# The second token tile's MoBA attention moved between the expert picks of the first tile

## The reference

```
x = x + rwkv7_time_mix(rms_norm(x))                       # block 1, layer A
k, v = shared keys and values of rms_norm(x) @ w_kv        # 16 heads of 64, block 1, layer B
q, gate = split(rms_norm(x) @ w_in)
o = softmax(mask(q k^T / 8)) v                             # causal: one MoBA block holds all 256 tokens
x = x + (o * silu(gate)) @ w_out
h = concat(16 meta tokens, x)                              # block 2
h = h + (sigmoid(g) * rg_lru(...) @ w_rnn + sigmoid(g') * mla_attention(...) @ w_att) @ w_out
h = h + peer(rms_norm(h))                                  # 8 heads x top 16 of 16384 experts, u and v rows gathered
out = rms_norm(h)[16:]
```

## Time and profile before

| | |
|---|---|
| median of 3 runs | 1422.13 us (1419.67 to 1423.77) |
| profiled execution, time | 1427.83 us |
| profiled execution, span | 1426.0 us |
| mean granted TensorE clock | 0.907 |
| busy in the span: TensorE, VectorE, ScalarE, GpSimd | 83%, 62%, 36%, 20% |
| bytes moved | 414.93 MB, of them 269.5 MB on the gathers' queue |

### The profile page before, as it was taken

One profiled execution on the slowest core, in us unless ns is written; L12 is line 12 of the kernel. 1 busy time (PEld: TensorE's weight loads), 2 busy tenths in 40 slices (PEclk: granted clock), 3 DMA queues, 4 the chain that ended last, 5 costly groups with the idle time before them and its releaser, 6 DMA issues.

```text
span 1426.0 us, 23109 instructions
## 1 busy us (share of the span) xinstructions
PE 1188.5 (83%) x8702; PEld 795.0 (56%) x8702; DVE 886.7 (62%) x2284; ACT 508.4 (36%) x1526; POOL 287.5 (20%) x269
## 2 busy tenths in 40 slices
PE   7999998999999999999897878986666665656564
PEld 4445798987479988998675544754122222222111
DVE  7526766556563563147585487566777787777654
ACT  1214222211262143122442476324344444344334
POOL 0000000000000000001231334322354344443440
PEclk9899999999999999999998989998678778787867
DMA  8344100243324586779999999999999999999995
GB/s 314 129 150 148 47 3 3 76 158 122 119 89 131 196 301 214 238 266 399 365 421 413 394 393 379 421 420 423 413 425 425 423 426 424 424 425 426 425 425 245
DMA packets 82960, 414.93 MB, mean 291 GB/s; under 512 B 10847, under 2 KB 15327, under 8 KB 49761
## 3 DMA queue, kind: packets, MB, share of 16 engines
q0 software_dynamic: 37152, 269.50, 45.6%
q1 hardware_dynamic: 45554, 143.69, 28.4%
q10 hardware_dynamic: 144, 0.26, 0.0%
HBM read 412.36 MB, written 1.06 MB: 290 GB/s over the span
## 4 chain that ended last, share of the span: by engine, by line
PE 46%; DMA 30%; DVE 6%; issue 3%; ACT 3%; POOL 2%; POOLq 0%; DVEq 0%; ACTq 0%
DMA row<-peer_in,arena 14%; PE bank L1893 12%; DMA arena<-peer_in,arena 12%; PE bank L2915 7%; DMA ring<-stream_in 4%; PE bank L1425 3%; PE bank L1505 2%; PE bank L2803 2%; PE bank L1482 2%; PE bank L846 2%; PE bank L2081 2%; PE bank L655 1%; PE bank L645 1%; POOL arena L3235 1%; DVE arena L3193 1%
## 5 line engine op out<-in xcount | busy, mean ns | idle before, releaser
L2915 PE MATMUL bank<-arena 128*64 128x512 f32 x808 | 321.6, 765 | 153.1 <-ACT arena L3050 153.1
L3193 DVE CUSTOM_DVE_ANT_0 arena<-arena 128x1024 f32<-128x1024 f32 x202 | 246.6, 1224 | 153.7 <-DMA arena<-peer_in,arena 150.8
L3235 POOL DMA_INDIRECT arena<-peer_in,arena x202 | 219.7, 1088 | 561.3 <-PE bank L2915 371.2
L2915 PEld LDWEIGHTS bank<-arena 128*64 128x64 f32 x808 | 76.5, 160 | 323.1 <-issue 319.7
L1893 PE MATMUL bank<-arena,ring 128*128 128x128 f32 (+1 forms) x1984 | 239.8, 281 | 13.3 <-DMA ring<-stream_in 11.7
L1893 PEld LDWEIGHTS bank<-arena,ring 128*128 128x128 f32 x1984 | 232.2, 194 | 27.6 <-issue 14.5
L3034 ACT ACTIVATE arena<-arena 128x2 f32<-128x2 f32 (+1 forms) x130 | 26.4, 203 | 393.6 <-DVE arena L3193 393.5
L3038 ACT ACTIVATE arena<-arena 128x1 f32<-128x1 f32 x256 | 85.4, 380 | 4.3
L3043 ACT ACTIVATE arena<-arena 128x1 f32<-128x1 f32 x256 | 84.1, 375 | 6.8 <-DVE arena L3199 6.4
L2803 PEld LDWEIGHTS bank<-arena,ring 128*128 128x128 f32 x512 | 65.8, 209 | 34.6 <-issue 29.3
L2915 PE MATMUL bank<-row,arena 128*64 128x512 f32 x112 | 71.5, 774 | 7.1 <-ACT arena L3050 7.1
(11 more groups left out here) (395 smaller groups left out, 1856.6 us busy)
## 6 DMA issues: line engine op xcount, KB each, us to landing
ring<-stream_in SPq DMA_DIRECT2D x243, 512.0 KB, 4.7
ring<-stream_in SPq DMA_DIRECT2D x16, 384.0 KB, 5.6
arena<-peer_in,arena POOLq DMA_INDIRECT x202, 19.9
row<-rows_in SPq DMA_DIRECT2D x4, 512.0 KB, 18.2
ring<-stream_in SPq DMA_DIRECT2D x16, 128.0 KB, 7.4
cst<-cst_in SPq DMA_DIRECT2D x1, 1900.0 KB, 17.0
row<-rows_in POOLq DMA_DIRECT2D x2, 512.0 KB, 6.0
cst<-rg_w_in SPq DMA_DIRECT2D x1, 1024.0 KB, 6.7
```

Source lines behind the costliest of these rows:

```text
L2915: return nc.tensor.matmul(core.banks[2 * t + b][rows_of(j), :], diag[i % ND], places[seat[i]][:, D + b * 512:D + (b + 1) * 512], start=Fal ...
L3193: ins = nc.vector.tensor_tensor_reduce(out=row, in0=row, in1=X2[t][i % 2], scale=STEEP, scalar=0.0, op0=ALU.mult, op1=ALU.add, accum_out=d ...
L3235: pool.indirect_dma_start(out=places[seat[i]], out_offset=None, in_=g.names["peer"], in_offset=bass.IndirectOffsetOnAxis(ap=index[:, i:i + ...
```

## The change

- The attention loop of `moba` does scores, transposes and weighted sums for the first tile only; one transpose bank now holds a pair of heads. The gate and the values are still projected there for both tiles. The output projection for the second tile goes, and with it the work that ran beside it.
- Keys, queries, values and gate that the second tile still needs are written to a DRAM tensor `spill` (four tiles of 512 KB, issued by GpSimd) and read back later (`bring`) into places that the first pass of `second_mix` has freed. ScalarE, VectorE and GpSimd wait for the four writes at the start of that pass.
- The second tile's attention becomes a generator `late_pass` for TensorE, ScalarE and VectorE, in `g.late`. `experts` draws on it ahead of `g.later`, from `START` on: 25 steps, then the output projection with `out_b` loaded a second time, then the norm for `second_mix`.
- `RATE` goes from 1.2 to 2.0. In unit 6 (picks 96 to 111) VectorE takes no step of choosing unit 8 in the first five pairs of picks and eight steps a pair after them (`LATE_ROUTE`).
- The place of the gates' weights is a seat from pick 0 up to pick 39 (`DROPPED`), so there are 7 seats then; from 40 to 63 there are 6, and the 1 MB of gates' weights is loaded again; 7 from 64 (`GATED`), 12 from 116.

The diff, cut to its core:

```diff
@@ moba, TensorE
         def scores(j):
-            banks = [claim(pe, ("s_b", 2 * j + p), p) for p in range(2)]
...
-                nc.tensor.matmul(banks[p][:, P:W3], qT[p][:, P:T], kT[p], start=True, stop=True).then_inc(*full(("s_b", 2 * j + p)))
+                nc.tensor.matmul(bank[:, 0:P], rotated["qb"][rows, 0, j, :], rotated["kb"][rows, 0, j, :], start=True, stop=True).then_inc(*full(key))
...
-        for m in range(KT):
-            key = ("out_b", 1, m)
-            bank = claim(pe, key)
-            project_out(bank[:, 0:P], m, 1).then_inc(*full(key))
...
+        def late_pass():
+            pe.wait_ge(brought.handle, 64)
+            copied(pe, ("vb", 1, 1))
+            for i in range(H + 9):
+                if i < H:
+                    late_scores(i)
+                if 5 <= i < H + 5:
+                    late_turn(i - 5)
+                if i >= 9 and i % 2:
+                    late_weigh((i - 9) // 2)
+                g.at["late", i] = g.now
+                yield ("late", i), 1
+            for n in range(2):
+                copied(pe, ("o_b1", n))
+            for m in range(KT):
+                late_out(m)
+                yield 1.0
+            yield ("out_b", 1, 1), 4
+            pe.wait_ge(squared_late.handle, 2)
...
+            g.at[key] = g.now
+            yield key, 4
+        g.late["pe"] = late_pass()
@@ moba, ScalarE
+        def late_pass():
+            for i in range(H + 9):
+                yield ("late", i), 1
+                if 6 <= i < H + 6:
+                    late_keep(i - 6)
+                if 2 <= i < H + 2:
+                    late_exps(i - 2)
...
@@ moba, VectorE
-            if m >= 6:
-                for j in range(4 * m - 24, 4 * m - 20 - (m == 7)):
-                    norm_first(j)
+        copied(dve, ("ss_c", 0))
+        lk(nc.vector.reciprocal(g.rstd_c[:, 0:first], g.rstd_c[:, 0:first]))
+        for j in range(KT):
+            nc.vector.scalar_tensor_tensor(out=g.second_in[0][:, j, :], in0=tiles(g.res, S)[:, j, 0:first], scalar=vec("norm1", j),
+                                           in1=g.rstd_c[:, 0:first], op0=ALU.mult, op1=ALU.mult).then_inc(*g.normed_c.up())
+        def late_pass():
+            dve.wait_ge(brought.handle, 64)
+            for i in range(H + 9):
+                yield ("late", i), 1
+                if 1 <= i < H + 1:
+                    mask(i - 1, 1)
+                if 3 <= i < H + 3:
+                    divide(i - 3, 1)
+                if i == 17:
+                    late_gated(0)
+            late_gated(1)
...
@@ moba, GpSimd
+        kept = [(rotated["kb"][:, 1, :, :], rotated_up, 4), (rotated["qb"][:, 1, :, :], rotated_up, 8)]
+        for n, (src, signal, count) in enumerate(kept):
+            pool.wait_ge(signal.handle, count)
+            pool.dma_start(tiles(g.spill[n], P), src).then_inc(*spilled.dma())
...
+    def bring(pool):
+        pool.wait_ge(spilled.handle, 64)
+        pool.wait_ge(g.rnn_ready[0].handle, 1)
+        pool.dma_start(late(0, D), g.spill[0]).then_inc(*brought.dma())
+        pool.dma_start(late(D, D), g.spill[2]).then_inc(*brought.dma())
+        filled(pool, ("att", 3, 0))
+        pool.dma_start(late(2 * D, D), g.spill[1]).then_inc(*brought.dma())
+        pool.dma_start(late(3 * D, D), g.spill[3]).then_inc(*brought.dma())
@@ second_mix, ScalarE and VectorE, first_pass
-            bank = filled(act, ("ss_c", 1))
-            nc.scalar.activation(rstd[:, NM + P:S], bank[:, 0:P], ACT.Sqrt, bias=g.eps[:, 0:1], scale=1.0 / D).then_inc(*free(("ss_c", 1)))
+            act.wait_ge(g.spilled.handle, 64)
...
+            dve.wait_ge(g.spilled.handle, 64)
@@ experts
-    START, RATE = -7, 1.2
+    START, RATE = -7, 2.0
+    LATE_ROUTE = 5
-    GATED, LATER = 16, 112
+    DROPPED, GATED, LATER = 40, 64, 116
...
         def front():
+            yield from g.late["pe"]
             yield from g.later["pe"]
...
+                steps = 5 if n == 0 else 3
+                if n == HP - 2:
+                    steps = 0 if q < LATE_ROUTE else 8
...
     def transfers(sp):
         sp.wait_ge(g.rnn_ready[0].handle, 1)
...
+        core.load_weights(sp, g.stream, core.slot_no["again", ("gr", 0)])
+        sp.wait_ge(used.handle, gates_wait)
+        g.load_gates(sp)
         core.load_weights(sp, g.stream, len(core.slots))
```

More of the change, by code:

```diff
@@ L1473, in _, with value_rows @@
                 rotate("kb", p - 1)
+        def value_rows(t, half, kp, slot):
+            for i in range(2):
+                k = 2 * kp + i
+                mm = nc.tensor.matmul(core.banks[core.bank_at["vb", t, half][0]][:, :], xn["kb"][:, k, t * P:(t + 1) * P],
+                                      slot[:, i * 512:(i + 1) * 512], start=k == 0, stop=k == KT - 1)
+            if kp == KT // 2 - 1:
+                mm.then_inc(*full(("vb", t, half)))
+            return mm
         for half in range(2):
-            banks = [claim(pe, ("vb", t, half)) for t in range(TT)]
+            ts = range(TT)
+            for t in ts:
+                claim(pe, ("vb", t, half))
             for kp in range(KT // 2):
@@ L1538, in weigh @@
[L1538 to L1545 removed]
+            copied(pe, ("pt_b", j))
@@ L1582, in _ @@
-        copied(pe, ("o_b", 3))
+                gate_part(next(parts))
+            if 1 <= i <= H // 2:
+                turn(i - 1)
+            if i < H // 2:
+                gate_part(next(parts))
+            elif i == H // 2:
+                copied(pe, ("o_b", 0))
+                for m in range(2):
+                    first_out(m, range(4))
+            if i == 2:
+                copied(pe, ("vb", 0, 0))
+                copied(pe, ("vb", 0, 1))
+            if i >= 2:
+                weigh(i - 2)
@@ L1583, in _ @@
+        for m in range(2, 4):
+            first_out(m, range(4))
+        copied(pe, ("o_b", 1))
         for m in range(4):
-            first_out(m, range(6, KT))
+            first_out(m, range(4, KT))
         for m in range(4, KT):
             first_out(m, range(KT))
-        def project_out(bank, m, t):
-            slot = core.weights(pe, ("out_b", m))
-            for k in range(KT):
-                mm = nc.tensor.matmul(bank, slot[:, k * P:(k + 1) * P], OT[:, k, t * P:(t + 1) * P], start=k == 0, stop=k == KT - 1)
-            return mm
@@ L1594, in _ @@
[L1594 to L1603 removed]
+        pe.wait_ge(g.summed_c.handle, 1)
@@ new lines, in _, with late_scores @@
+        bank = claim(pe, ("ss_c", 0))
+        nc.tensor.matmul(bank[:, 0:NM + P], cst("ones"), g.squares_c[:, 0, :], start=True, stop=True).then_inc(*full(("ss_c", 0)))
+        def late_scores(h):
+            key = ("s_b1", h)
+            bank = claim(pe, key, 4 + h % 2)
+            rows = slice(h % 2 * HD, (h % 2 + 1) * HD)
+            for kt in range(TT):
+                mm = nc.tensor.matmul(bank[:, kt * P:(kt + 1) * P], Q_LATE[rows, h // 2, :], K_LATE[kt][rows, h // 2, :], start=True, stop=True)
+            mm.then_inc(*full(key))
@@ new lines, in late_out @@
+        def late_out(m):
+            key = ("out_b", 1, m // 4)
+            source = ("again", ("out_b", m))
+            if m % 4 == 0:
+                claim(pe, key)
+            bank = core.banks[core.bank_at[key][0]]
+            slot = core.weights(pe, source)
+            for k in range(KT):
+                mm = nc.tensor.matmul(bank[:, m % 4 * P:(m % 4 + 1) * P], slot[:, k * P:(k + 1) * P], OT_LATE[:, k, :],
+                                      start=k == 0, stop=k == KT - 1)
+            if m % 4 == 3:
+                mm.then_inc(*full(key))
+                core.used_by(source, key)
+                g.at[key] = g.now
+            else:
+                mm.then_inc(*core.used_now(source))
@@ new lines, in late_pass @@
+        def late_pass():
[17 more added lines that the diff above has]
+            pe.wait_ge(squared_late.handle, 2)
+            key = ("ss_c", 1)
+            bank = claim(pe, key)
+            for m in range(KT):
+                mm = nc.tensor.matmul(bank[:, 0:P], cst("ones"), SQ_LATE[:, m, :], start=m == 0, stop=m == KT - 1)
+            mm.then_inc(*full(key))
+            g.at[key] = g.now
+            yield key, 4
@@ new lines, in _ @@
+        g.late["dve"] = late_pass()
+    @block.gpsimd
+    def _(pool):
+        kept = [(rotated["kb"][:, 1, :, :], rotated_up, 4), (rotated["qb"][:, 1, :, :], rotated_up, 8)]
+        for n, (src, signal, count) in enumerate(kept):
+            pool.wait_ge(signal.handle, count)
+            pool.dma_start(tiles(g.spill[n], P), src).then_inc(*spilled.dma())
+        for half in range(2):
+            copied(pool, ("vb", 0, half))
+        pool.dma_start(g.spill[2], V[0]).then_inc(*spilled.dma())
+        copied(pool, ("gateb", "pair", 3))
+        pool.dma_start(tiles(g.spill[3], P), tiles(gate, T)[:, :, P:T]).then_inc(*spilled.dma())
@@ L3000, in front @@
         def front():
+            yield from g.late["act"]
             yield from g.later["act"]
@@ L3166, in front @@
         def front():
```

(1 more changed line is left out.)

364 lines of the change are left out of this document (190 added, 174 removed).

## The result

The changed kernel took 1457.9 us (1457.5 to 1458.5) against 1421.3 for the kernel before: ratio 1.0256, 95% interval 1.0239 to 1.0274, 36.6 us slower. The prediction was 1425.5 with a range to 1437: it left the sign open, and the measured time lies 21 us above the range.

The account below looks back on a forecast made before the run. TensorE was taken to bound the kernel up to the first gather, DMA at 424 GB/s after it. Terms -20 + 12.4 + 8 + 3 = +3.4 on 1427.8, less 5.7, gave 1425.5 us; range 1413 to 1437.

Parts of the forecast that it names:

- The earlier start: Ahead of the first gather: shorter loop and dropped second-tile projection start it 20 us earlier, bounds 16 and 22.5.
- the loop: Attention loop: a pass takes 4.6 us instead of 5.96; gain 9.6 us, bounds 7.5 and 11.5.
- the bare norm: First tile's norm, no longer covered by the second tile's projection: 8.5 us; gain 10.7 us, bounds 8.5 and 11.
- Spill and bring: Four writes and four reads of 512 KB on GpSimd's queue: hidden, 0 us, bounds 0 and 4.
- The bytes: Behind the first gather: 5.24 MB more, `out_b` and gates, at 424 GB/s cost 12.4 us.
- The rest: Second tile's steps at places 60 to 85 and the choice of unit 8: together 0, bounds -4 and +4.
- A second thing points the same way: First picks: TensorE and ScalarE wait for VectorE's divisions and masks, holding up rows that free seats; part of the pick loss.
- the first picks: First 16 picks, paced by VectorE: DMA shortfall 15 us instead of 7.0, a loss of 8, bounds -2 and +14.
- The dense part: At doubled rate DMA stays the limit, but SP stops before `gr` until pick 34: 3 us lost, bounds 0 and 5.
- Seats stop turning: Slower rival, first 16 picks: 8.5 us a pair, a loss of 14; sum +11.4, 1433.5 us; chance 0.35 for all slower sums.
- Late steps hide: Faster rival: first picks run no worse than before, no stop at `gr`; sum -7.6, 1414.5 us; chance 0.28.
- The place named as the likeliest to make the prediction wrong: Picks 30 to 60, where six seats, doubled rate and the gates' second load meet: DMA may newly fall short there.

Follow-up runs that it names:

- after_skew1to3: The changed kernel with TensorE running drawn-in steps 1 pick ahead until the second tile's other attention, 3 from there; 1419.2 us, ratio 0.9986 to the kernel before.

## Why the prediction was wrong

**Right.** The earlier start: 20 us predicted, 20.8 measured; the loop 4.6 a pass (4.66), the bare norm 8.5 (9.4). Spill and bring hidden: the last spill was issued at 419.4 and landed in 3.4 us, well ahead of 440 (3.4 is the median of the four). The bytes: the page has 9.4 MB more than before, of which 5.24 lie behind the first gather, 12.4 us; with it the ledger above closes within 0.8 us. This core's DMA still ran at 422 GB/s from 1040 to 1380 (425 in after_skew1to3), so 424 holds for the bytes, and not the 358 GB/s that the Trainium skill's "DMA: Bandwidth & Descriptors", section "Bandwidth", names for a core with a busy neighbour. The rest: 0 predicted, -0.7 measured.

**Wrong: "A second thing points the same way", the bounds -2 and +14 on the first picks.** The prediction saw TensorE, 3 picks ahead, wait for VectorE, but only for divisions "one pair later", priced as a slower pace, 8.5 us a pair at worst. Between its gaps the pace was better than assumed: pairs of rows began at 641.0, 646.0, 652.3, then 664.8, 669.8, 674.3, 678.5, then 697.5. What the prediction lacked were the two gaps, 12.6 us to 664.8 and 19.0 to 697.5, at the gated heads, where TensorE waits for two or three dot products too many and the seats run out, so DMA drained. +20.1 instead of +8 (+15.5 with the prediction's cut at pick 16, just outside its bound of 14). Of the 27.1 us of shortfall up to 700, 13.1 lie in the run-up and the first pairs, the rest in the gaps. With TensorE one pick ahead the shortfall is 14.0 us up to 700; the prediction's sum over VectorE's work gave 15 up to pick 16, where this run has 11.7, 60 us in instead of 67.

**Wrong: "The dense part", 3 us with bounds 0 and 5.** It counted slots and bytes at the doubled rate and priced SP's stop by SP's own idle time. It didn't ask which due time that the old rate had hidden would now decide. The recurrence's hand-over (13.4 us of shortfall at 840 to 872) and SP's stop just ahead of the picks that TensorE needs (6.0 at 760 to 780) are the largest parts of +26.4. With TensorE one pick ahead it is 6.8 - 3.7 = 3.1 us, the predicted 3; and that is SP's stop, as predicted, for with an early stop or none the same stretch is short by 4.2 and 3.8 us instead of 6.8 (one trace each). So the two terms together were right as sums of work, 11 predicted and 10.1 measured in after_skew1to3; missing was a term for the order, put at nothing: 12.1 + 23.4 = 35.5 us.

**The rivals.** "Seats stop turning" had the right engine, place and sign and nearly the right size in its stretch, a loss of 14 against 15.5. Its pace is right only as a mean: the pairs took 8.1 us from 641.0 to 697.5, but as 4 to 6 us with two gaps, not 8.5 each. It had no such gap in the dense part, where it allowed 5. "Late steps hide" falls, since even with TensorE one pick ahead DMA is 14.0 us short up to 700. The place named as the likeliest to make the prediction wrong, picks 30 to 60, lies in the dense part, the larger half. The interleaving that the Trainium skill's "Perfetto Trace Analysis", section "Identifying Performance Opportunities", suggests pays nothing here even with TensorE one pick ahead: 20.8 us of start against 12.4 of bytes and 10.0 more shortfall (14.0 + 6.8 + 5.0 + 2.1 up to 1040, less 17.9) are +1.6, and the run gave no difference.

**Open.** Why START -4 loses 0.5%, two thirds of what RATE 2.0 costs the old kernel, and what most of the hand-overs cost by themselves: the runs show the price of TensorE's lead as a whole. No version beat the kernel before by more than its interval.

## What to carry to other kernels

When work is drawn into another loop with an offset for each engine, write down for every hand-over the iteration at which the producer and the consumer have it in their programs (its place less the engine's offset); where the consumer comes first, everything queued behind it waits, and if the distance uses up the buffers they stop turning, and the price is a drain, not the step's duration. Faster pacing moves hand-overs that were safe to the wrong side, so go through the due times again with each change of rate. One number that shifts an engine against the others is the cheapest test of it: here a shift of the whole pass took back 22 us, and the same shift, ended where it did harm, took back all 36.

## What the runs showed of the hardware

TensorE's granted clock fell in the run-up. Windows of the changed kernel around it, and four records of late scores at either level:

```profile
614.00:616.00 2.00, 1.11 (x10) 0.95 (x12) 1.83 (x10) 1.18 (x3) 1.59 (x2) 1.00 0.81 236
616.00:618.00 2.00, 0.32 (x6) 0.13 (x3) 1.83 (x10) 0.76 (x1) 1.39 (x3) 0.97 1.00 363
...
622.00:626.00 4.00, 4.00 (x15) 2.73 (x14) 3.82 (x16) 1.74 (x6) 0.59 (x1) 0.50 1.00 422
...
634.00:638.00 4.00, 4.00 (x12) 1.76 (x12) 3.76 (x13) 2.55 (x9) 0.00 (x0) 0.50 0.15 64
...
640.00:642.00 2.00, 2.00 (x19) 1.14 (x19) 1.93 (x8) 1.45 (x7) 0.00 (x0) 1.00 0.00 0
```
```profile
622.68 1.22 PE L1620 MATMUL bank<-arena 64*128 64x128 f32 x4
...
638.52 0.71 PE L1620 MATMUL bank<-arena 64*128 64x128 f32 x4
```

The engine was busy 1.43 us of the four from 614 to 618. From 618 to 638 the clock stood at 0.50, 1.2 GHz, though the engine was busy without a pause from 620 to 626; from 634 on it was busy again throughout, and by 640 the clock was back at 2.4. The same four records took 1.22 us at the one level and 0.71 at the other. The 9.0 us wait up to 664.0 shows it again: the weighted sum behind it took 1.12 us, the one at 669.3 took 0.66. So here a wait of TensorE for VectorE was followed by slower matmuls; what that adds to the 36 us no run separates.
